# A two-layer decoder step on one Trainium2 core: the last 17 pairs of up-projection tiles with seven block products in place of eight, their weight sums formed by adding DMAs

## What is computed

```python
def conv_ffn(x, prev, lp):
    T = x.shape[1]
    u = x @ lp["ffn_w_up"]
    gate, val = u[..., :D_FF], u[..., D_FF:]
    ext = jnp.concatenate([prev.astype(gate.dtype), gate], axis=1)
    conv = lp["ffn_conv_b"] + sum(ext[:, j:j + T] * lp["ffn_conv_w"][j] for j in range(CONV_WIDTH))
    h = jax.nn.gelu(conv) * val
    return h @ lp["ffn_w_down"], ext[:, -(CONV_WIDTH - 1):]
```

## Time and profile before

| | |
|---|---|
| median of 3 runs | 2004.49 us (2001.93 to 2006.17) |
| the profiled execution: its own time | 2001.52 us |
| its span, first to last instruction | 1999.7 us |
| TensorE busy, share of the span | 1937.3 us, 97% |
| VectorE, ScalarE, GpSimd busy | 1243.2, 732.4, 30.6 us |
| mean granted TensorE clock | 0.987 of full speed |
| up projection of layer 0 (from its fourth tile), of layer 1 | about 626 to 862 us, 1616 to 1852 us |

### The profile page before, as it was taken

The page is one execution under the profiler, slowest core; times in us unless marked ns, Lnnn a source line. Parts: engine busy times, 40 slices in busy tenths (PEclk is TensorE's granted clock), DMA queues, the critical chain, the costliest instruction groups (busy, mean ns, idle before and its releaser), DMA issues.

```text
span 1999.7 us, 53466 instructions
## 1 busy us (share of the span) xinstructions
PE 1937.3 (97%) x22496; PEld 1799.3 (90%) x22496; DVE 1243.2 (62%) x2070; ACT 732.4 (37%) x1394; POOL 30.6 (2%) x143
## 2 busy tenths in 40 slices
PE   8999999999999999999999999999999999999997
PEld 7999898766799999999999998887677999999997
DVE  3475868888638665542355767688786476656323
ACT  3223345563634222232232233545626342222321
POOL 0000000000000000000000000000000000000000
PEclk9999999999999999999999998999999999999999
DMA  5225443244222332232332264333442222233222
GB/s 218 90 80 164 149 138 128 65 119 132 86 89 64 96 96 86 95 95 95 101 142 85 75 204 140 118 107 93 121 126 72 78 85 94 86 96 96 95 96 89
DMA packets 153010, 214.29 MB, mean 107 GB/s; under 512 B 18497, under 2 KB 118338, under 8 KB 151362
## 3 DMA queue, kind: packets, MB, share of 16 engines
q1 hardware_dynamic: 134050, 200.38, 31.9%
q10 hardware_dynamic: 18720, 10.49, 1.8%
HBM read 202.58 MB, written 16.59 MB: 110 GB/s over the span
## 4 chain that ended last, share of the span: by engine, by line
PE 78%; DVE 13%; ACT 3%; DMA 2%; issue 2%; ACTq 1%; SPq 0%; DVEq 0%
PE ps L925 18%; PE ps L927 18%; PE ps L926 18%; PE ps L1315 4%; PE ps L1193 1%; DMA ring<-in_w 1%; PE ps L1286 1%; PE ps L1182 1%; PE ps L946 1%; PE ps L947 1%; DVE arena L2194 1%; DVE arena L2156 1%; PE ps L1279 1%; PE ps L1195 1%; DVE arena L2203 1%
## 5 line engine op out<-in xcount | busy, mean ns | idle before, releaser
L927 PE MATMUL ps<-hm_hi,ring_lo 128*128 128x260 f32 x1568 | 444.9, 284 | 0.0
L1882 DVE TENSOR_TENSOR ring_lo<-ring,ring_hi 128x1024 fp32r<-128x1024 f32 x130 | 159.3, 1225 | 306.3 <-ACT ring_hi L1479 304.1
L927 PEld LDWEIGHTS ps<-hm_hi,ring_lo 128*128 128x128 f32 x1568 | 296.9, 189 | 0.0
L925 PE MATMUL ps<-hm_hi,ring_hi 128*128 128x260 f32 x1008 | 285.5, 283 | 0.0
L926 PE MATMUL ps<-hm_lo,ring_hi 128*128 128x260 f32 x1008 | 284.6, 282 | 0.0
L1479 ACT ACTIVATE ring_hi<-ring 128x1024 fp32r<-128x1024 f32 x130 | 137.8, 1060 | 323.0 <-DMA ring<-in_w 314.6
L927 PE MATMUL ps<-hf_hi,ring_lo 128*128 128x260 f32 x704 | 198.9, 283 | 0.0
L927 PE MATMUL ps<-in_hi,ring_lo 128*128 128x260 f32 x704 | 198.8, 282 | 0.0
L925 PEld LDWEIGHTS ps<-hm_hi,ring_hi 128*128 128x128 f32 x1008 | 189.6, 188 | 1.8 <-issue 1.8
L926 PEld LDWEIGHTS ps<-hm_lo,ring_hi 128*128 128x128 f32 x1008 | 189.7, 188 | 0.0
L1882 DVE TENSOR_TENSOR ring_lo<-ring,extra_hi 128x1024 fp32r<-128x1024 f32 x64 | 78.4, 1225 | 152.8 <-ACT extra_hi L1479 151.1
(11 more groups left out here) (453 smaller groups left out, 4578.4 us busy)
## 6 DMA issues: line engine op xcount, KB each, us to landing
ring<-in_w SPq DMA_DIRECT2D x200, 512.0 KB, 3.6
extra<-in_kv_cmp SPq DMA_DIRECT2D x96, 128.0 KB, 2.3
arena<-in_kv_cmp SPq DMA_DIRECT2D x80, 128.0 KB, 2.6
slot<-in_kv_cmp SPq DMA_DIRECT2D x80, 128.0 KB, 2.4
out_win_old<-in_win SPq DMA_DIRECT2D x16, 511.0 KB, 4.4
slot<-in_k_sel SPq DMA_DIRECT2D x72, 64.0 KB, 2.0
extra<-in_k_sel SPq DMA_DIRECT2D x72, 64.0 KB, 1.9
arena<-in_v_sel SPq DMA_DIRECT2D x72, 64.0 KB, 2.1
```

The costliest lines, as they stand in the source:

```text
L925: mmul(out, wh, hi[:, k, cols], start=(k == 0), stop=False)
L927: last = mmul(out, wl, hi[:, k, cols], start=False, stop=(ci == len(chunks) - 1 and k == k1 - 1))
L1882: v.tensor_tensor(w_low(l, n), w_place(l, n), w_high(l, n), SUB).then_inc(S["w_lo"], 1)
```

## The change

The first five pairs (PAIRS = 5) of each up projection stay as they were. For each of the other 17 pairs (NG = 17) gate tile and value tile, the two halves of the input blocks and the two halves of the tokens make a 2 x 2 by 2 x 2 block product. It is formed with seven block products in place of eight (`SEVEN`, the order of TensorE): one product is 4 input blocks x 3 matmuls of 260 columns, 12 matmuls in one bank. A pair takes 84 matmuls in place of 96.

- The sums of activations (`t1` to `t4`, the "twins") are made once a layer, in pairs 2 to 4: ScalarE scales x (`scaled`, 8 instructions), VectorE adds (`twins`), both split (`twin_high`, `twin_low`).
- The sums of weights (`s1` to `s4`) are made in DRAM by GpSimd's DMAs: per layer 68 copies of 256 KB from DRAM to DRAM, then 34 adds onto them, then 17, then 17, with a wait for all that were issued between these four groups. Layer 0 starts them when the input projection is done, layer 1 when GpSimd has done its last copies of layer 0's up projection. GpSimd's copies of the last rows come behind them in its program; SP waits for them (`q_sum`) ahead of the first load of a sum.
- A pair's weights come in four parts: A (512 KB, straight from the weights), Z (512 KB), V (256 KB of sums and 256 KB of weights), F (256 KB), in two sets of buffers.
- Results of products are carried on in PSUM: ScalarE copies a bank into the next one (`seed` b and c) or into SBUF (p7, u4), and products add to it.
- EARLY is 4: 18 blocks of `hf` are split behind the loop in place of 11.
- Single-use semaphores of the input projection's side work are merged into three counters.

```diff
+PAIRS = 5
+NG = FT - PAIRS
+def seven_order():
+    out = [(0, "a11")]
+    for g in range(NG):
+        out += [(g, "s2"), (g, "a12"), (g, "s3"), (g, "s1")] + ([(g + 1, "a11")] if g + 1 < NG else []) + [(g, "a22"), (g, "s4")]
+    return out
+PAIR = {"a11": "A", "a12": "A", "s1": "Z", "s2": "Z", "s3": "V", "a22": "V", "s4": "F"}
...
-        EARLY = (HS - 14272) // TOK
+        EARLY = PAIRS - 1
...
+        def pair_free(eng, S, l, g, pair, first):
+            if g >= 2:
+                eng.wait_ge(S["q_pe"], SEVENS * l + SEVEN_AT[g - 2, LAST[pair]])
+            else:
+                eng.wait_ge(S["w_used"], C_UP + first)
...
-                    if n != C_UP + 2:
+                    if n != C_UP + 2 and not C_UP + 2 * PAIRS <= n < C_DOWN:
                         chunk(n)
+                    if n == C_UP + 2 * RING:
+                        pair_load("A", 0)
+                    if n == C_UP + 2 * PAIRS - 1:
+                        sp.wait_ge(S["q_sum"], 16 * SUM_DMAS * (l + 1))
+                        for pair in "ZVF":
+                            pair_load(pair, 0)
+                        for g in range(1, NG):
+                            for pair in "AZVF":
+                                pair_load(pair, g)
...
+                def product(q):
+                    g, name = SEVEN[q]
+                    pe.wait_ge(S["q_lo"], SPLIT_COUNT * l + TWINS + PREPARED_AT[PAIR[name], g])
+                    if name == "a11":
+                        if g < 2:
+                            pe.wait_ge(S["evac_v"], dense_n[0] - 2 + g)
+                        else:
+                            pe.wait_ge(S["q_gate"], 2 * (NG * l + g - 2) + 1)
+                    elif name == "s2":
+                        pe.wait_ge(S["q_seed"], SEEDS * l + 4 * g + 1)
+                    elif name == "s3" and g >= 2:
+                        pe.wait_ge(S["q_val"], 2 * (NG * l + g - 2) + 1)
+                    elif name == "s1":
+                        pe.wait_ge(S["q_seed"], SEEDS * l + 4 * g + 2)
+                    elif name == "s4":
+                        pe.wait_ge(S["q_seed"], SEEDS * l + 4 * g + 4)
+                    for k in range(HK):
+                        mmul(out, wh[:, w], hi[:, k, :], start=new, stop=False, skip_group_check=True)
+                        mmul(out, wh[:, w], lo[:, k, :], start=False, stop=False, skip_group_check=True)
+                        last = mmul(out, wl[:, w], hi[:, k, :], start=False, stop=(k == HK - 1), skip_group_check=True)
+                for q in range(SEVENS):
+                    product(q)
+                pe.wait_ge(S["q_gate"], 2 * NG * (l + 1) - 1)
+                pe.wait_ge(S["q_val"], 2 * NG * (l + 1))
...
+                    if m == 2:
+                        scaled()
+                    if m in (6, 7):
+                        twin_high(2 * m - 12)
+                        twin_high(2 * m - 11)
+                    if m >= 2 * PAIRS - 2:
+                        high("AZ"[m % 2], 0)
...
+                seed("b", 0)
+                high("V", 0)
+                for g in range(NG):
+                    if g + 1 < NG:
+                        high("A", g + 1)
+                    seed("c", g)
+                    if g:
+                        tap(g - 1)
+                    high("F", g)
+                    seed("p7", g)
+                    if g + 1 < NG:
+                        high("Z", g + 1)
+                    seed("u4", g)
+                    if g:
+                        gelu(g - 1)
+                    if g + 1 < NG:
+                        high("V", g + 1)
+                        seed("b", g + 1)
+                    else:
+                        split_w(C_DOWN, C_DOWN + 1, C_DOWN + 2)
+                tap(NG - 1)
+                gelu(NG - 1)
...
+                if l == 0:
+                    pool.wait_ge(S["evac_v"], N_IN)
+                else:
+                    pool.wait_ge(SL[l - 1]["ffn_t"], FT * l)
+                for first in (True, False):
+                    for n in range(NG):
+                        for i, src in (((0, val_a), (1, gate_a), (2, val_a), (3, gate_b)) if first else ((0, val_b), (2, gate_a))):
+                            to = w_sums[l, n, :, 512 * i:512 * (i + 1)]
+                            if first:
+                                pool.dma_start(to, part(n, *src)).then_inc(S["q_sum"], 16)
+                            else:
+                                pool.dma_start(to, part(n, *src), accum_op=ALU.add).then_inc(S["q_sum"], 16)
+                            done += 1
+                    pool.wait_ge(S["q_sum"], 16 * (SUM_DMAS * l + done))
+                for i in (1, 3):
+                    for n in range(NG):
+                        src = w_sums[l, n, :, 0:512] if i == 1 else w_sums[l, n, :, 512:1024]
+                        pool.dma_start(w_sums[l, n, :, 512 * i:512 * (i + 1)], src, accum_op=ALU.add).then_inc(S["q_sum"], 16)
+                        done += 1
+                    pool.wait_ge(S["q_sum"], 16 * (SUM_DMAS * l + done))
+                for i in range(FT):
+                    last_rows(i)
...
+                    if i == 2:
+                        conv_sample()
+                        twins()
+                    if i in (3, 4):
+                        twin_low(2 * i - 6)
+                        twin_low(2 * i - 5)
                     conv(i)
...
+                for pair in "AZV":
+                    low(pair, 0)
+                for g in range(NG):
+                    if g:
+                        gate_half(g - 1, 1)
+                    if g + 1 < NG:
+                        low("A", g + 1)
+                    if g:
+                        conv_second(g - 1)
+                    low("F", g)
+                    gate_half(g, 0)
+                    if g:
+                        conv_third(g - 1)
+                    if g + 1 < NG:
+                        low("Z", g + 1)
+                    else:
+                        split_w(C_DOWN, C_DOWN + 1, C_DOWN + 2)
+                    val_second(g)
+                    if g + 1 < NG:
+                        low("V", g + 1)
+                    if g:
+                        weigh(g - 1)
+                    val_first(g)
+                    if g:
+                        ffn_out(g - 1)
+                gate_half(NG - 1, 1)
+                conv_second(NG - 1)
+                conv_third(NG - 1)
+                weigh(NG - 1)
+                split_s(hf_lo, hf, hf_hi, FT - 1, EARLY)
+                ffn_out(NG - 1)
+                split_s(hf_lo, hf, hf_hi, FT, FT - 1)
```

352 lines of the change are left out of this document (289 added, 63 removed).

## The result

The changed kernel takes 2035.67 us (median of 4 runs, 2033.32 to 2041.06), the kernel before beside it 2004.22: a ratio of 1.0161, 95% interval 1.014 to 1.0181, so 31 to 32 us slower. The forecast was no change (2004). The result lies inside the range, in the rival "collisions at several places", which had 0.26.

A forecast was written before the change was run, and what follows sets the result against it. TensorE's matmuls were taken to bound the kernel (78% of the chain). Per layer -24.5 + 8.8 + 0.7 + 8.0 + 3.0 = -4.0, both layers -8.0; collisions +2 and +6 gave 0: 2004 us, range 1978 to 2042.

The forecast's parts named there:

- collisions at several places: Rival, chance 0.26: sums' transfers delay loads at layer 1's start and in attention units or chunks, +10 to +35, 2014 to 2040.
- The sums' DMAs: Step on GpSimd's 136 DMAs a layer: in time, costing only collisions, 2 in layer 0 and 6 in layer 1.
- The duration of the stream: Term for the sums' DMAs of a layer: 1.5 to 2 us each, 200 to 270 us, between 86 and 598.
- Layer 0's attention: Collision term: sums beside page loads at DMA share 0.41, units loaded one to two ahead; 0 to 10, taken as 2.
- The down projection: Layer 1's sums beside layer 0's down chunks: landing 3.6 us, could take some 8 (10.5 less 2.4 to split).
- layer 1's start: Collision term: sums meet the seven loads, chunk 4 lands some 5 us later, TensorE waits; 6, between 0 and 12.
- The ceiling and the pair loop: Up projection: 204 fewer matmuls save 24.5 us a layer, 49.0 in both; the loop runs at TensorE's pace without waits.
- The way in: Pairs 2 to 4, per layer: VectorE's twins work makes TensorE 8.8 us late, the first seed copy 0.7 more.
- The way out: End of pair loop, per layer: waits of 4.3 for value readings, 1.6 to 3 more, then 2.1; together about 8.
- Merged counters: Input projection's side work: same producers in the same order, so the merged semaphores cost nothing.
- VectorE pacing the loop: Rival, chance 0.06: 0.1 us more per VectorE instruction, at most 10 in the pair loop and 4 at the ends, about 2018.
- GpSimd shut out by VectorE: Mechanism within rival "Late sums" (0.08): GpSimd issues only while VectorE is idle, 136 DMAs take 544 us, 77 too many.

The follow-up runs named there:

- e1: The changed kernel without the sums' 136 DMAs a layer and SP's wait for them, parts loaded from plain weights; 1995.34 us, ratio 0.9975.
- e12: e11 plus e10's spreading of VectorE's work at the twins, the whole computation done; 2007.22 us, ratio 1.0031.
- e14: e13 with layer 1's first 34 adds, those beside layer 0's down projection, one in flight at a time; 2003.02 us, ratio 1.0015.
- e4: The changed kernel with the 68 adds of each layer turned into plain copies of the same bytes; 2025.81 us, ratio 1.0118.
- e13: e12 with layer 1's copies in layer 0's pair loop, a pause in layer 0's adds, 34 layer 1 adds beside the down projection; 2006.36 us, 1.0023.
- e7: The changed kernel with at most two of GpSimd's transfers in flight; 2033.43 us, ratio 1.0157.
- e10: e1 with VectorE's work for the twins spread one by one over pairs 1 to 4; 1991.96 us, ratio 0.9953.
- e16: e15 with VectorE's splits of the second and third down chunk moved behind the two value readings; 1991.67 us, ratio 0.9959.
- e11: The changed kernel with layer 0's sums begun behind its seven loads, layer 1's adds past its own, its copies two in flight; 2020.75 us, 1.0097.
- e15: e13 with all 68 adds of layer 1 behind the seven loads of that layer's start; 1999.42 us, ratio 0.9993.
- e8: The changed kernel with one of GpSimd's transfers in flight, layer 0's begun at the program's start; 2074.45 us, ratio 1.039.

## Why the prediction was wrong

The mechanism was named, and its size was off. The step that failed is "The sums' DMAs": the sum has 2 + 6 = 8 us for collisions, and with and without the transfers the kernels differ by 0.0186, 37 us. The other part, -8.0, came out at -5 (e1). In the step three terms failed:

- **The duration of the stream.** "I take 1.5 to 2 us each, 200 to 270 us." It was 2.9 us each, 388 to 400 us. The copies took 1.7 to 2.0 us each, as taken; the adds 3.6 to 4.1. The reason given, several in flight and half the size of the 4.4 us row, forgot that an add occupies the engines 2.2 times as long as a copy (1.95 against 0.89 us of all 16), and that in flight are at most seven copies but only three adds. At 270 us layer 0's stream would have ended at 442 us, just ahead of the costliest stretch. The bounds, 86 and 598 us, did hold it.
- **Layer 0's attention, "0 to 10, I take 2": 19.6 us, outside the term's own bounds.** "Units are loaded one to two units ahead" is no cover when a page load's landing goes from 2.3 to 5.7 or 6.9 us. TensorE waits 12.8 us in the stretch of `in_k_sel` and `in_v_sel` for loads and what follows them, and the clock over 440 to 560 us is 0.93 where it is 0.97 without the sums. The row with 2.25 us of waiting said that this stretch had no slack; the rival used it, the forecast did not.
- **The down projection, "two chunks' time, 10.5, less 2.4 to split", taken as cover, and layer 1's start, 6 (0 to 12).** Together 5.2 in layer 0's up and down projection (2.65 + the 2.6 that layer 1's gained) and 12.2 in layer 1's. The cover of 8 us is no full cover: with chunks landing in 4.3 us the stage is -0.4 and +3.0 over e1 (e12, e14), at 4.8 +5 to +7, at 6.5 +16 and +18 in single executions (e4, e13). The start's 6.2 us of waiting was sized well, from the share of 1.03; missed were 5 us more between 1080 and 1120, which wasn't traced to one load.

"DMA: Bandwidth & Descriptors" of the Trainium skill, section "Issuing engines are not separate DMA queues", which the prediction cited without a row to show it, is borne out by the landings of SP's loads beside GpSimd's transfers. The same page's section "SWDGE vs HWDGE vs iDMA" says that inside an engine GpSimd's queue and the hardware one are served in turn. One might take from it that a page load meets the same share of the engine whether two or seven transfers wait in GpSimd's queue. The trace doesn't agree for copies: with two in flight page loads land in 4.1 to 4.5 us in place of 5.7 to 7.2 (e7, 172 to 290 us). With two adds in place of three the landings are alike (4.4 to 4.8 us against 4.2 to 4.7).

**Right:**

- The ceiling and the pair loop. TensorE is busy in all of 140 us with a clock of 1.00 and no waits for seeds or splits (the line of e1 above). e1 gains 4.5 us in layer 0's two projections and 2.4 in layer 1's, where 4.0 were forecast for each.
- The way in, 8.8 + 0.7: the waits of the changed kernel in layer 0 are 2.9, 5.5 and 0.6. e10, where spreading took only 0.6 and 1.0 us of waiting away, speaks for the amount of VectorE's work and against its order, as the prediction had it.
- The way out, 8.0, of it 4.3, 1.6 to 3, and 2.1: waits of 3.9, 0.8 and 1.8, so 6.5. e16 shows the first one's cause.
- Merged counters, 0: the input projection of layer 0 ends at the same 171 us.
- Two small slips of the working changed nothing: ScalarE's pair adds up to 6.5 us, not 6.8, and 3.4 us at half clock lose 1.7 us, not 1.5.
- VectorE pacing the loop and GpSimd shut out by VectorE (two of the rivals) did not occur: VectorE's split of 1024 took 1.225 us in both kernels, and layer 0's copies were issued within 0.53 us each.

**The chances.** "Collisions at several places" (0.26) asked for "adds of over 2 us each" and gave +10 to +35; both came true. It should have been the forecast: its condition was the middle of my own bounds (86 and 598 us for 136 is 0.6 to 4.4 us each). Its price for layer 1's start, 12, was too high (7 measured there), and the units and chunks cost the rest, so that the total fits is in part luck.

**Open.** Why the stretch from 180 to 240 us costs 6 to 10 us beside adds in e11 and e12, and 3 to 4 even with the pause (e13 to e15, nothing in e16), wasn't traced to one load. Whether the loads wait in the engines or in DRAM, why e4's copies went faster, and how much of e13's 18 us is usual, stays open. What in an engine limits adds to three in flight no run shows. Sums on an engine in place of DMAs weren't tried.

## What to carry to other kernels

Work moved onto idle DMA engines isn't free while any stage has loads that arrive just in time: before placing a background stream, look for waits on DMA in the trace of before, however short, and for bursts of issues, and keep the stream out of these stretches or, for copies, few in flight. A stage with loads issued far ahead of their use takes it at an engine share of 0.89 for nothing (copies, e13 and e16). Price an accumulating transfer at twice a copy, and end the stream by its own measured length, not by a guess.

## What the runs showed of the hardware

- An adding DMA of 256 KB from DRAM to DRAM takes 31.2 engine-us against 14.2 of a copy (worked out from the shares of e4 and the changed kernel; 29.1 and 14.3 from stretches of the latter); the packets grew from 21760 to 30464 for the same 71.32 MB.
- GpSimd's issue of a copy takes 0.53 us; that of an add 0.81 to 1.48, with a median of 1.13, in the changed kernel.
- Alone in flight a copy lands in 3.7 us, an add of weights in 6.4 and an add of one sum onto another in 5.0 (e8), against 6.0, 7.0 and 6.9 with the queue full (changed kernel): a full queue brought the time for each from 5.2 to 2.9 us, no further. At most seven copies and three adds were in flight.
- Small and large transfers alike took two to two and a half times as long beside the sums. Over 440 to 560 us, at an engine share of 0.87, loads of 64 KB took 4.3 us in place of 1.9; over 172 to 300 us loads of 128 KB took 5.7 in place of 2.3 and copies of 511 KB 8.7 in place of 4.3. A chunk of 512 KB went from 3.5 to 4.3 beside two copies in flight, at a share of 0.68.
